# Latent attention over a paged cache: each page stored twice by the host and fetched in one transfer, VectorE's steps of two neighbouring pairs interleaved

## The reference, cut to what matters

```python
def _latent_attend(q_lat, q_pe, key_sets):
    for ckv, kpe, mask in key_sets:              # the past pages, then the own tokens
        s = (einsum('bthc,bsc->bhts', q_lat, ckv) + einsum('bthr,bsr->bhts', q_pe, kpe)) * scale
        ...
    probs = softmax(concatenate(scores, axis=-1), axis=-1)
    for ckv, _, _ in key_sets:
        part = einsum('bhts,bsc->bthc', probs[..., start:stop], ckv)   # summed over the sets
```

## Time and profile before

| | us |
|---|---|
| median of 3 runs | 1837.69 (1837.42 to 1839.45) |
| the profiled execution | 1840.06 |
| its span, first to last instruction | 1838.2 |
| TensorE busy in the span | 1757.1 (96%) |
| VectorE, ScalarE busy | 576.3 (31%), 451.2 (25%) |
| mean granted clock of TensorE | 0.985 of 2.4 GHz |

### The profile page before, as it was taken

The page is one execution under the profiler, slowest core; times in us unless marked ns, Lnnn a source line. Parts: engine busy times, 40 slices in busy tenths (PEclk is TensorE's granted clock), DMA queues, the critical chain, the costliest instruction groups (busy, mean ns, idle before and its releaser), DMA issues.

```text
span 1838.2 us, 27159 instructions
## 1 busy us (share of the span) xinstructions
PE 1757.1 (96%) x10832; PEld 1302.1 (71%) x10832; DVE 576.3 (31%) x1320; ACT 451.2 (25%) x979; POOL 113.1 (6%) x190
## 2 busy tenths in 40 slices
PE   7999899999999999999999989999999999999997
PEld 5676567777767767777766755676777677777775
DVE  1431266332022253330034324652320240633201
ACT  3233233132031231110132342321311332311101
POOL 1003000010010010000010030000100100100000
PEclk9999999999999999999999999999999999999999
DMA  8522322165337433343164133221733473333431
GB/s 309 155 97 82 137 77 85 67 235 192 115 137 292 171 120 138 137 142 114 65 244 160 29 88 149 83 82 47 292 133 139 150 307 122 113 136 137 142 114 49
DMA packets 66767, 256.75 MB, mean 140 GB/s; under 512 B 8529, under 2 KB 36626, under 8 KB 39378
## 3 DMA queue, kind: packets, MB, share of 16 engines
q1 hardware_dynamic: 54722, 199.52, 30.8%
q0 software_dynamic: 11360, 54.21, 7.9%
q10 hardware_dynamic: 560, 1.30, 0.2%
HBM read 245.80 MB, written 9.19 MB: 139 GB/s over the span
## 4 chain that ended last, share of the span: by engine, by line
PE 89%; DVE 5%; ACT 2%; issue 2%; DMA 1%; ACTq 0%; POOL 0%; DVEq 0%; POOLq 0%
PE banks L789 41%; PE banks L818 16%; PE banks L740 6%; PE banks L773 6%; PE banks L796 5%; PE banks L847 4%; PE banks L737 4%; PE banks L745 3%; PE banks L1048 1%; DVE work L1912 1%; PE banks L1017 1%; PE banks L1439 1%; ACT work L1523 1%; PE banks L1458 1%; DMA weight_ring<-in_w 1%
## 5 line engine op out<-in xcount | busy, mean ns | idle before, releaser
L789 PE MATMUL banks<-h_normed,weight_ring 128*128 128x288 f32 x1888 | 459.4, 406 | 1.1 <-ACT h_normed L1523 1.1
L789 PEld LDWEIGHTS banks<-h_normed,weight_ring 128*128 128x128 f32 x1888 | 358.6, 190 | 100.5 <-ACT h_normed L1523 1.5
L818 PE MATMUL banks<-h_normed,weight_ring 128*128 128x288 f32 x1024 | 280.9, 418 | 4.6 <-ACT values_by_token L1695 4.6
L818 PEld LDWEIGHTS banks<-h_normed,weight_ring 128*128 128x128 f32 x1024 | 189.2, 191 | 64.6 <-issue 8.5
L789 PE MATMUL banks<-work,weight_ring 128*128 128x288 f32 (+1 forms) x960 | 226.8, 399 | 1.8 <-issue 1.8
L789 PEld LDWEIGHTS banks<-work,weight_ring 128*128 128x128 f32 x960 | 182.2, 190 | 46.1 <-issue 2.6
L1523 ACT ACTIVATE work<-banks 128x512 f32<-128x512 f32 (+7 forms) x206 | 94.2, 457 | 283.2 <-PE banks L745 74.2
L1912 DVE TENSOR_TENSOR squares<-squares 128x288 f32<-128x288 f32 (+2 forms) x40 | 20.3, 508 | 329.4 <-ACT squares L1561 329.2
L773 PE MATMUL banks<-h_normed,weight_ring 128*128 128x288 f32 x448 | 116.3, 411 | 0.0
L773 PEld LDWEIGHTS banks<-h_normed,weight_ring 128*128 128x128 f32 x448 | 83.1, 191 | 28.6 <-issue 8.1
L847 PE MATMUL banks<-h_normed,weight_ring 128*128 128x288 f32 x288 | 81.7, 445 | 19.8 <-DMA weight_ring<-in_w 13.6
(11 more groups left out here) (302 smaller groups left out, 1703.2 us busy)
## 6 DMA issues: line engine op xcount, KB each, us to landing
weight_ring<-in_w SPq DMA_DIRECT2D x171, 1024.0 KB, 4.8
work<-in_mem_k POOLq DMA_DIRECT2D x12, 1024.0 KB, 11.0
work<-in_mem_v POOLq DMA_DIRECT2D x12, 1024.0 KB, 9.4
work<-in_pool SPq DMA_DIRECT2D x128, 80.0 KB, 2.1
weight_ring<-in_pool SPq DMA_DIRECT2D x64, 80.0 KB, 2.0
projected<-in_mem_k POOLq DMA_DIRECT2D x4, 1024.0 KB, 24.9
projected<-in_mem_v POOLq DMA_DIRECT2D x4, 1024.0 KB, 6.2
weight_ring<-in_pool POOLq DMA_DIRECT2D x32, 80.0 KB, 2.2
```

The lines of the kernel that those rows point to most:

```text
L789: last = mm(ps[:, bank, 0:width], block_of(first + k), rhs(k), start=k == 0, stop=k == n - 1)
L818: last = mm(ps[:, BANK[g], 0:N], block_of(t[2] + k), H[:, k, :] if t[0] == "gate" else O[:, 2 * n + k, :], start=k == 0, stop=k == t[3] - 1)
```

## The change: what it does

The host stores each page as 128 rows of 288 numbers: the latents, the same latents transposed, and the rotated keys transposed in pieces of 32. A page is one transfer of 144 KB. TensorE's 160 page transposes of a layer, ScalarE's 40 copies and VectorE's 8 packings go. The latent scores read the transposed half directly (four matmuls of 512 columns in four column groups); the rotated keys are added by 16 matmuls of 128 columns, their operand in runs of 32.

`fill` has 8 more blocks ahead of the page section (16 for 12 at L941 and L973) and 32 in it; `mix` runs to 16 in it (11 before, and 13 behind `mla_o`). TensorE's and VectorE's steps of a pair are interleaved with those of the next, the odd pair's maxima lie in bank 0 or 4, its scores in banks of their own. The mLSTM's steps of ScalarE and VectorE are moved ahead. Pages 3, 5 and 7 go through POOL, 0, 1, 2, 4 and 6 through SP, into three places reused: 4 after the sums of 0, 5 after the sums of 1, 6 and 7 after the fourth sum, 7 also after the last block of `fill`. Slots N_IN and N_IN+1 wait for the fourth sum, N_IN+2 for the last.

```diff
+        whole = groups(work, 0, 11)
+        lent, o_half, first = groups(slots, 3 * SLOT * P, 3), groups(of, 4 * N, 1), groups(slots, 0, 4)
+        kv = [whole[0:4], whole[4:8], lent + o_half, whole[8:11] + first[:1],
+              whole[0:4], whole[4:8], whole[8:11] + o_half, first]
...
+        slot_after = {N_IN: 3, N_IN + 1: 3, N_IN + 2: 7}
+        S_BANK = (4, 5, 0, 1)
+        TOP_BANK = (2, 0, 2, 4)
...
+        def cache(eng, layer, b, parts=range(4)):
+            at_b = [(p, eng.value_load(pages[0:1, b * PAGES + p:b * PAGES + p + 1], min_val=0, max_val=POOL - 1))
+                    for p in range(PAGES) if p % 4 in parts]
+            for p, page in at_b:
                 src = t_in["pool"][layer, bass.ds(page, 1)].rearrange("g p a -> (g p) a")
+                eng.dma_start(kv[b][p % 4][:, p // 4, :], src).then_inc(S(f"kv_full{b}"), 16)
...                                                     # SP
+                                sp.wait_ge(*before("post_ffn_done", KD))
+                        for b, parts in {4: [(0, range(4))], 7: [(1, range(4))], 10: [(2, (3,))]}.get(s, []):
+                            cache(sp, layer, b, parts)
+                    sp.wait_ge(*at("gemm_done", slot_done(N_IN - 4)))
+                    cache(sp, layer, 2, (0, 1, 2))
+                    sp.wait_ge(*at("mla_pv", 1))
+                    cache(sp, layer, 4)
                     for s in range(N_IN, NSLOT):
                         if s in slot_after:
                             sp.wait_ge(*at("mla_pv", slot_after[s] + 1))
                         slot(s)
+                        if s == N_IN + 1:
+                            sp.wait_ge(*at("mla_pv", 4))
+                            cache(sp, layer, 6)
...                                                     # POOL
+                    cache(pool, layer, 3, (0,))
+                    pool.wait_ge(*at("mla_ol", 2))
+                    cache(pool, layer, 3, (1, 2))
+                    pool.wait_ge(*at("gemm_done", slot_done(N_IN - 3)))
+                    cache(pool, layer, 3, (3,))
+                    pool.wait_ge(*at("mla_pv", 2))
                     cache(pool, layer, 5)
+                    pool.wait_ge(*at("gemm_done", slot_done(N_IN - 1)))
+                    pool.wait_ge(*at("mla_pv", 4))
                     cache(pool, layer, 7)
...                                                     # TensorE
                     def scores(b):
+                        pe.wait_ge(*at(f"kv_full{b}", 16 * PAGES))
+                        out = [ps[32 * j:32 * j + 32, bank, :].rearrange("p (i k) -> p i k", i=4) for j in range(4)]
                         for j in range(4):
+                            mm(out[j], m_qz[:, g, 32 * f:32 * f + 32], turned(b, j), start=f == 0, stop=True, skip_group_check=True)
+                        for k in range(0, P, 32):
+                            for j in range(4):
+                                last = add(out[j][:, :, k:k + 32], m_qpz[:, g, P * f + k:P * f + k + 32], rotary(b, j))
...                                                     # shares and values are attend's two halves
+  scores(0) scores(1) fill(4) maxima(0) scores(2) maxima_back(0) scores(3) shares(0) fill(4)
+  maxima(1) values(0) maxima_back(1) fill(4) outputs(0) fill(2) shares(1) fill(4) values(1) fill(4) outputs(1) fill(6)
+  scores(4) fill(4) scores(5) mix(3) maxima(2) mix(5) maxima_back(2) mix(6)
+  scores(6) shares(2) scores(7) maxima(3) values(2) maxima_back(3) mix(8) outputs(2) mix(10)
+  shares(3) mix(12) values(3) mix(14) outputs(3) mix(16)          # one call a line in the program
...                                                     # VectorE
+                    for g in (0, 2):
+                        page_tops(g)
+                        query_tops(g)
+                        tops_back(g)
+                        shares_turned(g)
+                        page_tops(g + 1)
+                        query_tops(g + 1)
+                        latent_sums(g)
+                        query_outputs(g)
+                        tops_back(g + 1)
+                        shares_turned(g + 1)
+                        latent_sums(g + 1)
+                        query_outputs(g + 1)
```

More of the change, by code:

```diff
@@ L403, in program @@
         m_po = sqf[:, 1152:1152 + NS]
[L404 to L412, removed]
+        m_selr = sqf[:, 1184:1216]
+        m_sums = sqf[:, 1216:1218]
+        m_recs = sqf[:, 1218:1219]
+        m_tops = sqf[0:1, 1220:1220 + NS]
+        m_row = sqf[0:1, 1252:1252 + P]
+        m_pot = sqf[0:NS, 1380:1380 + P]
+        m_os = sqf[:, 1508:1764]
         prf = PR[:, :, :].rearrange("p a b -> p (a b)")
@@ L1080, in _ @@
-                    g = NB // 2 - 1
-                    mix(2)
-                    maxima(g)
+                    scores(0)
+                    scores(1)
+                    fill(4)
+                    maxima(0)
+                    scores(2)
+                    maxima_back(0)
+                    scores(3)
+                    shares(0)
+                    fill(4)
+                    maxima(1)
+                    values(0)
+                    maxima_back(1)
+                    fill(4)
@@ L1084, in _ @@
+                    outputs(0)
+                    fill(2)
+                    shares(1)
+                    fill(4)
+                    values(1)
+                    fill(4)
+                    outputs(1)
+                    fill(6)
+                    scores(4)
+                    fill(4)
+                    scores(5)
                     mix(3)
-                    maxima_back(g)
+                    maxima(2)
+                    mix(5)
+                    maxima_back(2)
                     mix(6)
-                    attend(g)
@@ L1088, in _ @@
-                    mix(10)
-                    outputs(g)
-                    mix(11)
+                    scores(6)
+                    shares(2)
+                    scores(7)
+                    maxima(3)
+                    values(2)
+                    maxima_back(3)
+                    mix(8)
+                    outputs(2)
+                    mix(10)
+                    shares(3)
+                    mix(12)
+                    values(3)
+                    mix(14)
+                    outputs(3)
@@ L1091, in _ @@
+                    mix(16)
                     pe.wait_ge(*at("mla_ols", NB // 2))
@@ L1629, in _ @@
                         late_out()
+                    wait("ml_abs")
+                    step(A(l_t[0:4, :], l_t[0:4, :], ACT.Exp))
+                    step(A(l_t[0:4, :], l_t[0:4, :], ACT.Ln, bias=one[0:4, :]), "ml_log")
                     wait("mla_ql")
```

190 lines of the change are left out of this document (60 added, 130 removed).

## The result

The kernel after takes 1852.64 us (median of 7 runs, 1849.56 to 1860.53), the kernel before 1835.48 (7 runs, 1833.51 to 1839.45): ratio 1.0098, 95% interval 1.0077 to 1.0119. It is 17 us slower, where 2.5 us, no measurable change, were forecast. The 1852.64 lie just inside the range of all the forecast's cases (1821 to 1853) and outside that of its main case (1832 to 1848). The profiled execution took 1857.07 (span 1855.4) against 1840.06 (span 1838.2); the difference, 17.2 in the span, is that of the medians, so the two profiles can be set against each other.

What follows compares the result with a forecast made beforehand. TensorE was taken to set the pace. Sections of 4.0 + 1.2 + 95.0 = 100.2 us against 98.7 and 96.2, less 3.0 behind each, gave 2.5 us longer: 1842.6 profiled, 1840 predicted as median, range 1821 to 1853.

Steps and rivals of the forecast that it cites:

- main case: Whole kernel: the prediction's own sum, near no change, with a range of 1832 to 1848 us and a chance of 51%.
- rival 4: Page scores: operands in runs of 32 are dear, 4.0 us more for each scores, 20 a layer: 1880; 4%.
- the late copy: Ahead of the page section: `fill` waits 1.2 us for ScalarE's copy of the fifth late projection, behind the prompt's exponentials.
- three blocks of `mix` fewer: Behind the page section: 16 blocks done against 13, so 3.0 us back in each layer.
- Slot N_IN+2 waits for the last sums: Weight slot on SP's queue: released later, its reader 20 us away, so charged at nothing.
- Page set 4 at 45.9: Wait at `scores(4)`: the set is there 45.9 us after `scores(0)`, SP issuing from 30.4, at 340 GB/s; 7.0 idle.
- 8.7 + 9.5 + 2.2 = 20.4: POOL's reads, issues and landing for page set 7 after the last late block, putting it at 73.0 us.
- The clock behind page set 7: From `scores(7)` to the output projection: 2.3 us charged for the low clock after the wait.
- rival 3: Page fetching: the two queues take rate from each other, 286 GB/s, 8.6 us in all: 1849; 18%.
- Rival 1: Page sections: pages come sooner, at 435 GB/s, and half the clock loss goes: 1828; 22%.
- Rival 2: Page sections: no wait for pages at all, 69 us a layer, 59 us gained: 1779; 5%.
- Rival 5: Interleaved pairs: it does nothing, waits for exponentials stay about 1 us each; in the sum, no chance of its own.

Runs made afterwards that it cites:

- e1: Kernel after, with the table reads of page sets 3 to 7 done ahead of the waits for their memory: 1815.75 us, ratio to before 0.9898.
- e6: Kernel after, with SyncE's weight slots N_IN+2 and later held until the mLSTM's states have landed: 1849.21 us, ratio 1.0061.
- c9: c8 with weight slot N_IN+1 behind page set 6 on SyncE's queue in place of ahead of it: 1796.42 us, ratio 0.9784.
- e11: c8 with 80 KB in place of 144 KB a transfer for page sets 4 to 7: 1791.57 us, ratio 0.976.
- e3: Kernel after, with 80 KB in place of 144 KB a transfer for page sets 4 to 7, as many transfers: 1847.89 us, ratio 1.0061.
- c12: c9 with two of ScalarE's three copies of late projections between the exponentials of the prompt's halves: 1795.95 us, ratio 0.9768.
- e2: Kernel after without fetching page sets 4 to 7; those sequences work on the pages of sequences 0 and 1: 1799.76 us, ratio 0.9811.
- c8: Kernel after with early table reads, SyncE's further ahead, last late blocks ahead of scores(4), mLSTM states ahead of slot N_IN+2: 1799.98 us, ratio 0.9792.
- e10: c8 with the pairs handled one by one in place of interleaved: 1806.55 us, ratio 0.9824.
- e5: e1 with the pairs handled one by one in place of interleaved: 1819.37 us, ratio 0.9904.
- e4: Kernel before, with page transposes and copies only for the first sequence, the other 140 and 35 a layer left out: 1815.88 us, ratio 0.9907.

## Why the prediction was wrong

**What held.** Sizes and order of the new work: scores 1.75 (forecast 2.0), runs of 32 cost nothing extra (rival 4 out), 1.15 for the late copy (1.2), 0.90 for ScalarE's copy behind the output projection (0.9). The mechanism too: TensorE waits at `scores(3)`, `(4)`, `(6)` and `(7)`, 25.7 and 25.2 us a layer against some 23, set by reads, issues and landing behind each wait; e1 shows it by moving only the reads. One sign of being wrong did appear, over 400 GB/s with both queues (417 from 172 to 176), but with two weight slots among the pages. Page set 7 was there at 75.4 after `scores(0)` (forecast 73.0), the tail from there took 21.8 in the first layer (22.0).

**What failed**, 14.7 us between +2.5 and +17.2:

1. *"Behind the section three blocks of `mix` fewer are left in each layer: 3.0 back"* and *"Slot N_IN+2 waits for the last sums, its reader is 20 us away. All at nothing"*: 6.3 us, the largest. The slot was costed by its own reader. What stood behind it was another queue's transfer: the later release puts 4 MB of weights right in front of the mLSTM's states, whose last load took 9.3 us to land in place of 4.2. The part behind the section became 3.3 longer, not 3.0 shorter. VectorE's wait for the states is shown by e6 to come from this order, and the twelve layers of each kind put its price at 1.9 us a layer, so at some 4 of the 6.3. What is left goes with the clock in this part, 0.83 and 0.82 against 0.90 and 0.86 before; its cause stays open.

2. *Page set 4 at 45.9*, and *8.7 + 9.5 + 2.2 = 20.4* for page set 7: set 4 came at 47.8 (175.76 less 128.00) and set 7 2.4 and 2.5 late, 4.9 in both layers. SP's first issue came 1.1 later than I had it (31.5 behind `scores(0)`, forecast 30.4): 0.4 by the first sums, the rest between these and the issue, 9.4 us where I had 8.7 for the reads. From there to the last page of set 4 it took 0.8 longer. The 340 GB/s that I took were slightly high for pages alone (314 from 164 to 168, 327 from 1084 to 1088), and the two slots issued at 168.10 drew on the rate while page set 4 was still on its way (398 and 417 with them); I had charged them nothing. Which of the two took the 0.8 was not tried alone; c9 and e11 show slots and rate at work where the reads no longer hide them. From the last block to page set 7, POOL's reads, issues and landing took 21.6 and 21.2 us, not 20.4; the shorter stretch at low clock between gave 0.7 and 0.2 back.

3. *The clock behind page set 7, 2.3 in each layer*: the second layer lost 3.5 more. From set 7's arrival to the mLSTM's transposes, 22.0 by the forecast, the same work took 21.8 and 25.5 us. The windows behind the wait, second layer:

```profile
1120.00:1124.00 4.00, 3.23 (x40) 1.79 (x40) 0.00 (x0) 0.00 (x0) 0.00 (x0) 0.50 0.01 3
1124.00:1128.00 4.00, 2.93 (x45) 2.32 (x37) 1.34 (x4) 0.00 (x0) 0.00 (x0) 0.50 0.00 0
1128.00:1132.00 4.00, 4.00 (x46) 2.42 (x39) 0.48 (x3) 0.00 (x0) 0.00 (x0) 0.50 0.01 4
1132.00:1136.00 4.00, 4.00 (x12) 2.88 (x10) 0.71 (x3) 0.96 (x3) 0.00 (x0) 0.53 0.00 0
```

In the first layer the clock was 0.59 in 204 to 208 and back at 1.00 from 208. What decides stays open. The same tail behind a wait of over 3 us took 21.8 and 21.5 in e6, 25.8 and 23.5 in e3, 21.8 and 21.5 in c9, 23.7 and 23.4 in e11, 25.5 in c12's second layer: it varies from one execution and layer to the next, and 22.0 was near its lower end, so that the first layer's 21.8 agrees with the forecast in part by luck. After's own runs range over 11 us, before's over 6.

6.3 + 4.9 + 3.5 are the 14.7; the 0.2 by which the first layer's tail was shorter are lost in rounding.

**The rivals.** By number rival 3 (1849) came nearest, but not by its mechanism: both queues together moved more than 286 GB/s, and e3 gave 4.7 us for 44% fewer bytes. Rival 1 needed sooner pages and half the clock loss: the pages came later and the clock was low for longer. Rival 2's price was right in kind: without the late sets the time is 1799.8 (e2), with set 3 still waited for, where 1779 had none. Rival 5, that the interleaving does nothing, is probably wrong: handling the pairs one by one cost 6.6 us on c8 (e10, intervals just touching) and 3.6 on e1 (e5, not told apart). The transposes' worth, 36 us of arithmetic (35.2 by the forecast's own 17.6 a layer), was not there in full in the old order: 140 of 160, some 31 us, gave 19 (e4).

**Two stated figures against the trace.** The windows of pages and slots run at 398 and 417 GB/s, past the 358 that the Trainium skill gives as what binds transfers from HBM ("DMA: Bandwidth & Descriptors", section "Where 436 GB/s comes from"). The section takes it as one of two cores' share of 716; here one core runs alone, and as a bound for it the trace contradicts the figure. Sixteen reads take 8.84 us, 0.55 each; the same page's floor of some 600 ns a read (section "Latency and other measured facts") is a little above that, so the trace does not bear it out as a floor.

## What to carry to other kernels

When work is removed from the pacing engine, list what it had hidden: here transfers and VectorE's steps. Before judging that data come too late for their bytes, look at what the queue does between its wait and its first issue, and move that ahead of the wait: it needs no memory. And when a transfer is moved, ask not only who reads it but which transfers of other queues it now runs beside.

## What the hardware showed that was not expected

- A read of a table number costs its queue 0.55 us (8.84 for 16), twice what its own record shows, and nearly as much as the issue of the transfer that it is for (9.37 for 16, c9).
- Rows of 1152 bytes came at 314 GB/s (after, 164 to 168, share 1.02) and at 373 and 395 (c8, 164 to 172, shares of 1.06 and 1.08), rows of 640 at 256 and 274 with shares of 0.93 and 0.95 (e3). By these I estimate that a page of 80 KB takes the DMA engines some 30 to 40% less time than one of 144 KB, for 44% fewer bytes. That the issues bound e3's windows in part is not excluded.
- A wait of 8 to 9 us was followed by some 4 us at 1.2 GHz in the first layer (203.4 to 207.3) and by 15 in the second (1120.8 to 1135.7), with the same work behind it.
